# A ring of expert weights: its first slot released and refilled in two halves, the two halves of its fourth slot counted as they land

## What is computed

```python
def moe_ffn(h, router_w, router_b, w_gu, b_gu, w_down, b_down):
    ...
    def expert_block(args):
        xblk, e = args
        gu = xblk @ w_gu[e] + b_gu[e]
        g, up = gu[:, :D_FF_2], gu[:, D_FF_2:]
        g = jnp.minimum(g, SWIGLU_LIMIT)
        up = jnp.clip(up, -SWIGLU_LIMIT, SWIGLU_LIMIT)
        act = (up + 1.0) * (g * jax.nn.sigmoid(SWIGLU_ALPHA * g))
        return act @ w_down[e] + b_down[e]
    ...
```

## Time and profile before

| | us |
|---|---|
| median of three runs | 1956.32 |
| the profiled execution, whole | 1955.71 |
| the profiled execution, its span | 1953.9 |
| TensorE busy in the span | 1876.0 (96%) |
| VectorE busy | 717.8 (37%) |
| ScalarE busy | 256.1 (13%) |
| GpSimd busy | 203.1 (10%) |
| DMA queue of SP, share of the 16 engines' span | 69.0% |
| read from HBM | 556.35 MB |

### The profile page before, as it was taken

One profiled execution on the slowest core, in us unless ns is written; L12 is line 12 of the kernel. 1 busy time (PEld: TensorE's weight loads), 2 busy tenths in 40 slices (PEclk: granted clock), 3 DMA queues, 4 the chain that ended last, 5 costly groups with the idle time before them and its releaser, 6 DMA issues.

```text
span 1953.9 us, 22912 instructions
## 1 busy us (share of the span) xinstructions
PE 1876.0 (96%) x8306; PEld 922.1 (47%) x8306; DVE 717.8 (37%) x1524; ACT 256.1 (13%) x501; POOL 203.1 (10%) x393
## 2 busy tenths in 40 slices
PE   8999999999999999999799999999999999999996
PEld 4466767744667777555433333233233333333332
DVE  3553111145626871494622232232232323322323
ACT  1411000014110000221211011011011101110111
POOL 0200000002007868220000000000000000000000
PEclk9999999999999999998699999999999999999999
DMA  8143343241458864221699999999997499999995
GB/s 307 65 173 130 136 172 129 108 185 65 173 233 325 326 233 173 86 87 55 258 417 429 428 429 428 427 429 429 429 429 294 204 429 428 427 429 428 429 429 236
DMA packets 40911, 558.10 MB, mean 286 GB/s; under 512 B 4535, under 2 KB 5431, under 8 KB 6365
## 3 DMA queue, kind: packets, MB, share of 16 engines
q1 hardware_dynamic: 40380, 556.06, 69.0%
q10 hardware_dynamic: 480, 1.37, 0.2%
HBM read 556.35 MB, written 1.06 MB: 285 GB/s over the span
## 4 chain that ended last, share of the span: by engine, by line
PE 68%; DMA 23%; DVE 6%; ACT 1%; issue 1%; SPq 0%; ACTq 0%; DVEq 0%; POOLq 0%
DMA ring<-in_exp_w 23%; PE PS L1716 15%; PE PS L2001 15%; PE PS L1444 8%; PE PS L1735 8%; PE PS L2032 6%; PE PS L1621 3%; PE PS L1758 1%; PE PS L1752 1%; PE PS L1905 1%; PE PS L1987 1%; PE PS L2009 1%; DVE tT L1363 1%; DVE tT L1360 1%; DVE tb L1364 1%
## 5 line engine op out<-in xcount | busy, mean ns | idle before, releaser
L2001 PE MATMUL PS<-ring,tb 128*64 128x512 f32 x2176 | 483.9, 598 | 22.7 <-POOLq L2131 19.8
L2001 PEld LDWEIGHTS PS<-ring,tb 128*64 128x64 f32 x2176 | 150.9, 137 | 351.1 <-issue 297.2
L1716 PE MATMUL PS<-hT,ring 128*128 128x256 f32 x1376 | 300.6, 380 | 0.0
L1716 PEld LDWEIGHTS PS<-hT,ring 128*128 128x128 f32 x1376 | 261.7, 190 | 42.4 <-issue 8.6
L2032 PE MATMUL PS<-ring,tb 128*64 128x512 f32 x1088 | 241.0, 595 | 3.7
L1444 PE MATMUL PS<-ring,hT 128*128 128x512 f32 (+2 forms) x448 | 187.6, 561 | 1.9 <-ACT hT L415 1.9
L1360 DVE TENSOR_SCALAR tT<-PS 128x512 f32<-128x512 f32 x34 | 23.5, 692 | 401.9 <-PE PS L2009 401.9
L1735 PE MATMUL PS<-ring,tT 128*128 128x512 f32 x352 | 154.7, 593 | 0.0
L2032 PEld LDWEIGHTS PS<-ring,tb 128*64 128x64 f32 x1088 | 77.7, 137 | 145.1 <-issue 144.1
L1444 PEld LDWEIGHTS PS<-ring,hT 128*128 128x128 f32 x448 | 81.9, 193 | 71.4 <-issue 59.3
L1069 DVE TENSOR_TENSOR tT<-PS,tT 128x512 f32<-128x512 f32 x22 | 15.2, 692 | 270.2 <-PE PS L1716 270.2
(11 more groups left out here) (441 smaller groups left out, 1570.1 us busy)
## 6 DMA issues: line engine op xcount, KB each, us to landing
ring<-in_exp_w SPq DMA_DIRECT2D x192, 2048.0 KB, 21.2
ring<-in_w_gate_up SPq DMA_DIRECT2D x22, 2048.0 KB, 8.6
ring<-in_ada_w SPq DMA_DIRECT2D x12, 2048.0 KB, 9.2
ring<-in_w_in_part SPq DMA_DIRECT2D x10, 2048.0 KB, 10.2
ring<-in_w_down SPq DMA_DIRECT2D x10, 2048.0 KB, 7.3
ring<-in_w_out SPq DMA_DIRECT2D x6, 2048.0 KB, 8.7
ring<-in_w_in SPq DMA_DIRECT2D x4, 2048.0 KB, 8.0
ring<-in_w_in_part SPq DMA_DIRECT2D x2, 1608.0 KB, 11.7
```

The source lines that it names most:

```text
L1716: ins = pe.matmul(PS[:, 4 + 2 * (i % 2) + part, 256 * f:256 * f + 256], wt[:, k, 256 * part + 128 * f:256 * part + 128 * f + 128], hT[:, k ...
L2001: ins = pe.matmul(PS[64 * h:64 * h + 64, b, :], xg[:, o:o + 64], ring[:, s, w:w + 512], start=k == 0, stop=False, skip_group_check=True)
```

## The change

Slot 0 is refilled in two halves of 1 MB. In the loop, the first half (block k = 0) is issued as soon as TensorE has done the products of k = 0 of the last item of the expert before, which it counts on a new semaphore `m_fh`; the second half waits for `freed[0]` as the whole slot did. Both halves count on `landed[0]`, and GpSimd waits for both at once. Slot 3 is loaded in two halves too, issued together when `freed[3]` allows; the first counts on a new semaphore `m_lh`, the second on `landed[3]`. GpSimd passes each of them on to `m_w`, which now counts 7 an item, and TensorE waits for the first half before k = 6 and for the second before k = 7. The loads of the first expert are cut in the same way.

```diff
             def expert(e, items_before):
 
                 for slot in range(RING):
+                    src = a["exp_w"][e, slot]
+                    if slot == 0 and not isinstance(e, int):
+                        sp.wait_ge(g.m_fh, items_before)
+                        sp.dma_start(ring[:, slot, 0:2048], src[:, 0:2048]).then_inc(landed[slot], 16)
                     sp.wait_ge(freed[slot], items_before + USES_BEFORE[slot] + 1)
-                    sp.dma_start(ring[:, slot, :], a["exp_w"][e, slot]).then_inc(landed[slot], 16)
+                    if slot == 0:
+                        if isinstance(e, int):
+                            sp.dma_start(ring[:, slot, 0:2048], src[:, 0:2048]).then_inc(landed[slot], 16)
+                        sp.dma_start(ring[:, slot, 2048:4096], src[:, 2048:4096]).then_inc(landed[slot], 16)
+                    elif slot == 3:
+                        sp.dma_start(ring[:, slot, 0:2048], src[:, 0:2048]).then_inc(g.m_lh, 16)
+                        sp.dma_start(ring[:, slot, 2048:4096], src[:, 2048:4096]).then_inc(landed[slot], 16)
+                    else:
+                        sp.dma_start(ring[:, slot, :], src).then_inc(landed[slot], 16)
...
                 for s in range(4):
-                    pe.wait_ge(g.m_w, n * RING + s + 1)
                     for kk in range(2):
                         k = 2 * s + kk
+                        if kk == 0 or s == 3:
+                            pe.wait_ge(g.m_w, n * (RING + 1) + s + kk + 1)
...
+                        if k == 0:
+                            ins.then_inc(g.m_fh, 1)
                     ins.then_inc(freed[s], 1)
...
                     if c % 4 == 0:
-                        pe.wait_ge(g.m_w, n * RING + s + 1)
+                        pe.wait_ge(g.m_w, n * (RING + 1) + s + 2)
...
                 for slot in range(RING):
-                    pool.wait_ge(landed[slot], (e + LOADS_BEFORE[slot]) * 16 + 16)
+                    if slot == 0:
+                        pool.wait_ge(landed[slot], e * 32 + LOADS_BEFORE[slot] * 16 + 32)
+                    elif slot == 3:
+                        pool.wait_ge(g.m_lh, e * 16 + 16)
+                        pool.sem_inc(g.m_w, 1)
+                    if slot > 0:
+                        pool.wait_ge(landed[slot], (e + LOADS_BEFORE[slot]) * 16 + 16)
                     pool.sem_inc(g.m_w, 1)
```

More of the change, by code:

```diff
@@ L324, in program @@
             s_c12 s_c13 s_c14 s_c15 s_na s_nb s_rope s_t1 s_e1 s_rs s_rd s_rp s_rq s_rg s_rm s_g1 s_g2 s_g3 s_ws s_gp s_gm s_mg s_mge
-            s_mr s_mre s_wo s_xa s_xt2 s_hd2 s_ha2 s_dg s_rb s_re s_gu s_gr s_pf s_th s_actv s_dn s_df s_out r_par r_ssm r_row r_glu
-            d_acc d_ps d_ev u_p u_ea qk_p qk_e vo_p vo_e u_de u_e u_bu u_bd u_sc u_pd u_c u_y y_g1 y_g2 y_gd u_pl u_pa m_bg m_p m_xg m_xr
+            s_mr s_mre s_wo s_xa s_xt2 s_hd2 s_ha2 s_dg s_rb s_re s_gu s_gr s_pf s_th s_actv s_dn s_df s_out r_par r_ssm r_row
+            d_acc d_ps d_ev u_p u_ea qk_p qk_e vo_p vo_e u_de u_e u_bu u_bd u_sc u_pd u_c u_y y_g1 y_g2 y_gd u_pl u_pa m_fh m_lh m_p m_xg m_xr
             m_xt m_xge m_w m_hw m_pw m_pwe m_gu m_gs m_th m_a m_at m_ate m_y m_ye m_s m_sd m_es m_dve m_f m_fs pe2 act2 dve2""".split()
@@ L366, in _ @@
                     sp.wait_ge(g.d_ev, MODS)
-                    sp.dma_start(post, a["s5_glu_w"]).then_inc(g.r_glu, 16)
+                    sp.dma_start(post, a["s5_glu_w"]).then_inc(g.r_row, 16)
                     continue
@@ L641, in _ @@
             for half in range(2):
-                act.dma_start(bgu[32 * half:32 * half + 32, :], a["exp_b_gu"]).then_inc(g.m_bg, 16)
+                act.dma_start(bgu[32 * half:32 * half + 32, :], a["exp_b_gu"]).then_inc(g.r_par, 16)
             def mixed_squares(t):
@@ L1886, in gated @@
                 return ins
-            pe.wait_ge(g.r_glu, 16)
+            pe.wait_ge(g.r_row, 48)
             pe.wait_ge(g.y_gd, 1)
@@ L1978, in _ @@
             turn_gathered(1)
-            pe.wait_ge(g.m_bg, 32)
+            pe.wait_ge(g.r_par, 48)
             pe.wait_ge(g.dve2, DVE2["m_tab"] + 1)
```

## The result

| | before | after |
|---|---|---|
| median of 16 runs, us | 1956.35 | 1959.55 |
| range, us | 1955.69 to 1958.18 | 1957.61 to 1962.64 |
| ratio of after to before, 95% interval | | 1.0018 (1.001 to 1.0026) |
| span of the profiled execution, us | 1953.9 | 1956.2 |

The change makes the kernel 3.2 us slower (0.16% between the medians). That is under the 0.2% that I called tellable, but the interval of the ratio lies wholly above 1, so the kernel did get slower. The forecast was 1954.9 with a range to 1959.0, so both the direction and the range missed.

A forecast was written before the change was run, and what follows sets the result against it. Load bandwidth was taken to bound the expert loop's long stretches, TensorE its start and the doubled experts. Terms 1.43 + 1.43 + 1.2 - 2.7 = 1.36, rounded 1.4 us sooner: 1956.32 - 1.4 = 1954.9 us, range 1952.8 to 1959.0.

The forecast's parts named there:

- What bounds the kernel: Expert loop: loads' bandwidth in long stretches, 29.37 us an expert; TensorE until about 1152 us and around doubled experts 17, 18.
- (a): Slot 3 counted by halves: next work starts 1.43 us sooner, counting at the first doubled item and the last item.
- (b): Slot 0 given back by halves: 1.2 us sooner at the loads' first restart, 0 at the last, nothing in steady stretches.
- (c): Price of half loads in 8 KB packets: 0.05 us per split slot, bounds 0 and 0.13, 54 slots, -2.7 us.
- rival 2: Extra loads in a full queue cost the engines unseen time; split pays only under 0.075 us; 1960.4 us, chance 0.10.
- The fixed cost of about 2 us: Per transfer: exposed, 62 more transfers would add 124 us; taken as hidden under the load ahead, no chance of its own.
- (d): SP's extra issues, GpSimd's extra wait and increment, TensorE's wait before k = 7, renamed semaphores: at most -0.1 us, taken as 0.
- Rival 3: Slot 3's early count brings nothing, through late landings or engines drifting apart: 1957.8 us, within 0.2%, chance 0.13.

## Why the prediction was wrong, step by step

- **What bounds the kernel.** Right. The loop is at the bandwidth limit in the long stretches, slot 3's landing ended them, and experts 17 and 18 are the doubled ones. The restarts are where TensorE's time counts.
- **(a), the count by halves: +1.43 twice.** Right, with its limit: after the change slot 2 is late next, by the 1.28 us in the rows above. The traces give 1.46 at the first doubled expert and 1.47 at the end.
- **(b), the early half of slot 0: +1.2 at the start, 0 at the last restart.** This is the step that failed in its mechanism. I took 7.7 us from issue to landing for a fixed number, and left out that the early half also changes when slot 1's and slot 4's loads meet the engines. The 7.7 us at expert 19 weren't even those of an empty queue: the engines were busy for 2.1 to 2.8 us more when that load was issued. Loads issued less than 2.2 us before the first engine fell idle took up to 10.6 us. The last restart cost 2.1 us in the profiled execution. The start's 1.2 came in that one and was lost in the other trace, with 1.2 more.
- **(c), the price of a split slot: 0.05 us.** The mechanism was right, the size was not: by the landings 0.154 to 0.159 us an expert over two slots, so 0.08 a slot. That is inside the bounds of 0 and 0.13, and just past the break-even at 0.075 that rival 2 named. Over 54 slots the difference is 1.6 us. The prediction took the earlier trace rows as the nearer in kind and set aside. In the trace of before the 8 KB packets of the earlier trace rows take 0.3096 us on average (155 of them) and those of the earlier trace rows 0.3137 (203), and in the loop of the kernel after they take 0.3136: the row set aside was the right one. The 0.316 worked out from the earlier trace rows was too high, because its share also holds one packet of 16 KB and the small ones. A further transfer in a full queue, rival 2's mechanism, costs nothing that can be seen: one load in 8 KB packets goes at the same pace as two halves. The fixed cost of about 2 us that the prediction takes from the Trainium skill (DMA: Bandwidth & Descriptors, Anatomy of one DMA) is given there for loads that GpSimd issues, and these are SP's; nothing in the sum hung on it.
- **(d), the rest: 0.** Nothing in the traces speaks against it. TensorE's items without waits for loads still take 27.55 us.

The sum with the measured terms is 1.46 + 1.47 + 1.2 - 54 x 0.08 - 2.1 = -2.3 us, and the profiled execution's span grew by 2.3. Of the 3.7 us between this and the forecast, (b) stands for 2.1 and (c) for 1.6: with (c) alone put right the change would have come out within 0.2 us of nothing, and the loss comes from (b). Where the first restart is lost too, as in the second trace, it is -4.7; the median, 3.2 us slower, lies between the two. How often the first restart is lost the unprofiled runs don't tell.

The rivals had one mechanism for the slower side, and it was the wrong one. That the time from issue to landing was a measured number from two places only, and that the change makes loads arrive at a moment that the trace of before doesn't show, should have been a rival of its own. Rival 3 named a drift of the engines, but judged it by the steady stretches, where the steps are even; at the restarts they are not (1.7 us between the engines at slot 3 of expert 1, before the change).

## What to carry to other kernels

Where loads are queued deep and set the pace, giving a buffer back sooner gains nothing but at a restart, and cutting a load costs packets: weigh the gain, which comes once or twice, against the price, which every load pays. Counting the last load before a wait by halves is worth up to half of the work on it (1.46 of 1.74 us here, because the load before it is late next), but only where a stretch hands its time on; cut it there alone (here the last expert: 1.9 us between the medians, 1.5 in the traces). The price of a load isn't a number but depends on when it arrives: before moving an issue, see what the queues are doing at that moment.

## What the hardware showed that I had not expected

- **8 KB packets cost some 2% over 16 KB packets in the steady stream.** 0.3136 us against 0.6149/2 (mean durations over 1200:1440 in the trace of the kernel after), which would be 0.10 us for a load of 2 MB; the landings give 0.08, whether it is one load or two. The Trainium skill (DMA: Bandwidth & Descriptors, Specifications) gives 512 bytes as enough for line rate; at this resolution, 8 KB isn't yet quite there.
- **A load of 64 partitions runs at half the rate, and can slow the whole loads around it.** Alone it went at 197 GB/s, with 437 for the whole load behind it. With the engines 28 us apart, rows of 16 KB took 1.18 us instead of 0.616 in nearly all loads; with the engines together about a third of the rows were slow, as many as lie in the cut slots. The kernel took 24% longer. The Trainium skill (DMA: Bandwidth & Descriptors, Rules for kernel authors) says of two transfers to disjoint halves of the partitions not to bother, as they share the same engines; the trace shows that here they did real harm. Why its packets take twice as long, and why the others' then do, was not tried.
- **The time from issue to landing depends on the moment.** For slot 4 at the restarts it was 7.6 to 8.0 us where the load came 2.0 to 2.3 us before the first engine fell idle (experts 18 and 19), 8.5 to 9.1 at 1.2 to 1.4 us, 7.7 to 9.0 at 0.4 to 0.5 us, 7.5 to 8.2 behind that moment, and up to 10.6 with engines out of step. Not every load at a bad moment lost: slot 4 of expert 1 took 7.5 and 7.6 us at 0.7 and 0.8 us ahead in two of the kernels with the early half.
- **Executions of one kernel differ by some 3 us ahead of the loop.** In the second trace of the changed kernel, TensorE was granted its lower clock of 1.2 GHz for the 17 us up to 977.3, where the first had it at 2.4 GHz for 3.4 us of that time and from 975.2 on (as the kernel before did). Slot 1 of expert 1 was issued at 983.0 there, and at 980.0 in the first. The mean granted clock tells part of it: the kernel before ran in 1955.5 to 1956.8 us where it was 0.987 and in 1957.2 to 1959.2 where it was 0.983, but anywhere from 1955.8 to 1959.6 where it was 0.984. A change of a microsecond has to be read from the traces, place by place.
